# Attention scores in three 64-row products, two row halves at a time

## The reference

```
s_c = q . kc * scale    kc: 63 compressed keys (blocks of 32 tokens, stride 16), mask cmp_end <= t
s_s = q . ks * scale    selected blocks; 16 of 16 blocks are taken, so all tokens <= t
s_w = q . kw * scale    the last 512 tokens
o   = gate0 * softmax(s_c) vc + gate1 * softmax(s_s) vs + gate2 * softmax(s_w) vw
```

## Time and profile before

| | |
|---|---|
| median of 3 runs | 2566.24 us (2565.07 to 2568.8) |
| profiled execution | 2569.07 us, its span 2567.3 us |
| TensorE (PE) busy | 2495.6 us, 97% of the span |
| weight loads (PEld) busy | 2046.7 us, 80% |
| VectorE (DVE) busy | 1711.0 us, 67% |
| ScalarE (ACT) busy | 1053.7 us, 41% |
| GpSimd (POOL) busy | 82.3 us, 3% |
| mean granted TensorE clock | 0.990 |

### The profile page before, as it was taken

How to read it: one execution, slowest core, us unless ns; L and a number is a source line. 1 busy time by engine, 2 the same in 40 slices (tenths; PEclk the granted TensorE clock), 3 DMA queues, 4 the chain that set the end, 5 groups by cost and what they waited for, 6 DMA issues and landing times. The chain is left out here.

```text
span 2567.3 us, 47240 instructions
## 1 busy us (share of the span) xinstructions
PE 2495.6 (97%) x19440; PEld 2046.7 (80%) x19440; DVE 1711.0 (67%) x2707; ACT 1053.7 (41%) x1823; POOL 82.3 (3%) x122
## 2 busy tenths in 40 slices
PE   8999999999899999789999998999999999999998
PEld 7788888888777778777888886877787888888887
DVE  6876676687545455478788777634457866776676
ACT  4322223445433343456655554533443322223443
POOL 0000000000000000011121110000000000000000
PEclk9999999999999999989999999999999999999999
DMA  4323324665432267922212114511121333235464
GB/s 149 101 83 119 118 82 145 207 201 156 99 110 91 69 209 233 256 64 52 56 39 51 46 44 145 200 58 33 66 74 54 128 110 118 89 99 205 143 196 145
DMA packets 279268, 297.91 MB, mean 116 GB/s; under 512 B 75442, under 2 KB 209840, under 8 KB 279088
## 3 DMA queue, kind: packets, MB, share of 16 engines
q1 hardware_dynamic: 276208, 292.59, 36.3%
q10 hardware_dynamic: 2880, 2.75, 0.3%
HBM read 208.67 MB, written 81.36 MB: 113 GB/s over the span
## 5 line engine op out<-in xcount | busy, mean ns | idle before, releaser
L1141 PE MATMUL f_ps<-hi,f_wh 128*128 128x512 f32 x672 | 262.4, 391 | 4.1 <-DVE f_wl L847 4.1
L1143 PE MATMUL f_ps<-hi,f_wl 128*128 128x512 f32 x672 | 262.2, 390 | 0.0
L2586 PE MATMUL f_ps<-hi,f_ahead_h 128*128 128x512 f32 x392 | 163.9, 418 | 0.8 <-PEq L72 0.8
L2588 PE MATMUL f_ps<-hi,f_ahead_l 128*128 128x512 f32 x392 | 153.6, 392 | 0.0
L2587 PE MATMUL f_ps<-one_lo,f_ahead_h 128*128 128x512 f32 x392 | 153.4, 391 | 0.0
L1141 PE MATMUL f_ps<-f_t3h,f_t2h 128*128 128x512 f32 x392 | 152.5, 389 | 0.0
L1142 PE MATMUL f_ps<-f_t3l,f_t2h 128*128 128x512 f32 x392 | 152.5, 389 | 0.0
L1143 PE MATMUL f_ps<-f_t3h,f_t2l 128*128 128x512 f32 x392 | 152.5, 389 | 0.0
L1141 PEld LDWEIGHTS f_ps<-hi,f_wh 128*128 128x128 f32 x672 | 126.6, 188 | 31.3 <-DVE f_wl L847 5.0
L1143 PEld LDWEIGHTS f_ps<-hi,f_wl 128*128 128x128 f32 x672 | 126.5, 188 | 26.3
L1142 PE MATMUL f_ps<-one_lo,f_wh 128*128 128x512 f32 x352 | 137.0, 389 | 0.0
(11 more groups left out here) (586 smaller groups left out, 6595.4 us busy)
## 6 DMA issues: line engine op xcount, KB each, us to landing
act<-one_y SPq DMA_DIRECT2D x30, 512.0 KB, 3.5
f_work<-act SPq DMA_DIRECT2D x30, 512.0 KB, 3.7
act<-y SPq DMA_DIRECT2D x30, 512.0 KB, 3.6
arena<-act SPq DMA_DIRECT2D x30, 512.0 KB, 3.6
one_y<-in_w_in SPq DMA_DIRECT2D x25, 512.0 KB, 4.6
early<-in_ffn_w_gate SPq DMA_DIRECT2D x11, 1024.0 KB, 6.2
early<-in_ffn_w_up SPq DMA_DIRECT2D x11, 1024.0 KB, 8.7
f_raw<-in_ffn_w_gate SPq DMA_DIRECT2D x10, 1024.0 KB, 6.4
```

The costliest lines, as they stand in the source:

```text
L1141: nc.tensor.matmul(out, wh, xh, start=start, stop=False)
L1143: return nc.tensor.matmul(out, wl, xh, start=False, stop=stop)
L2586: nc.tensor.matmul(dense_ps[:, b, cols], w_hi[:, b, k, :], hi[:, k, cols], start=(k == 0), stop=False)
L2588: mm = nc.tensor.matmul(dense_ps[:, b, cols], w_lo[:, b, k, :], hi[:, k, cols], start=False, stop=(k == KD - 1))
```

## The change

1. **Scores.** Tokens of a key block are split into two halves of 64, one in rows 0 to 63 and one in rows 64 to 127 of the key tile; high and low parts of the keys lie side by side in the free dimension. A score step is now three products (high x high, high x low, low x high), each given twice, once for the upper and once for the lower 64 rows, with n x 64 columns each. The low x low product is dropped. The scores of the two halves land in two banks of PSUM.
2. **Masks, minimum, exponential.** VectorE writes masked scores into a new tile `raw` (two buffers), still in two halves; ScalarE's exponential reads it and writes the probabilities in token order. The minimum of step s waits for the exponential of step s - 2; the wait for a free probability tile moves from VectorE to ScalarE (for the compressed part it stays).
3. **Compressed keys.** 64 (63 and a masked one) instead of 63 in a tile `near`, both heads of the pair side by side: one transpose instead of two per unit, one copied block instead of two, and two 64-row products with values that stand in both row halves.
4. **Loads.** `load_keys` issues 16 DMAs with runs of 256 bytes instead of 4; `kc` comes in 4 DMAs instead of 2 and waits for a memset, `vc` in 2 instead of 1.
5. **Recurrence.** VectorE writes T0 = result * m_one at once, L and its mask are gone, and GpSimd has one operation less per chunk.
6. **Planner.** New costs, the moved wait, and a tiling of its own, "rows", for the scores.

```diff
@@ joint_plan
-        event(("score", s), "pe", 0.113 * n + 0.1 + extra, s and ("max", s - 1))
-        event(("max", s), "dve", 0.25 + 1.1 * us + extra, ("score", s), u >= 2 and ("bank", FIRST_FILL[u - 1] - 1))
-        event(("exp", s), "act", 0.4 + us + 2 * extra, ("max", s), s and ("exp", s - 1))
+        event(("score", s), "pe", 0.085 * n + 0.1 + extra / 2, s and ("max", s - 1))
+        event(("max", s), "dve", 0.25 + 1.1 * us + extra, ("score", s), s >= 2 and ("exp", s - 2),
+              u >= 2 and k >= 2 and ("bank", FIRST_FILL[u - 1] - 1))
+        event(("exp", s), "act", 0.4 + us + 2 * extra, ("max", s), s and ("exp", s - 1), u >= 2 and ("bank", FIRST_FILL[u - 1] - 1))
...
-                event(("masked", c), "pool", 4.6, out_of(name))
+                event(("masked", c), "pool", 3.9, out_of(name))
...
-        return e[0] == "values" and "columns" or e[0] == "rw" and e[2] not in ("mean", "var") and "corners" or "whole"
+        return e[0] == "score" and "rows" or e[0] == "values" and "columns" or e[0] == "rw" and e[2] not in ("mean", "var") and "corners" or "whole"
@@ load_keys
-        src = rot[row:row + 2 * DH, :].rearrange("(g d) t -> d g t", d=DH)
-        sp.dma_start(hi[w * CH:(w + 1) * CH, 2 * n:2 * n + 2, :].bitcast(F32), src).then_inc(keys_in, 16)
+        for g in range(2):
+            src = rot[row + g * DH:row + (g + 1) * DH, :].rearrange("d (t r c) -> d r t c", r=2, c=CH)
+            for r in range(2):
+                sp.dma_start(keys_of(hi, n)[r * CH:(r + 1) * CH, w, g].bitcast(F32), src[:, r]).then_inc(keys_in, 16)
@@ score
-                for key, first, n, col in parts:
-                    for m in range(0, max(n, 1), 4):
-                        width = min(4, n - m) * P if n else NB + 1
-                        at = s_ps[:, col + m * P:col + m * P + width]
-                        keys = key[:, g, (first + m) * P:(first + m) * P + width]
-                        nc.tensor.matmul(at, q[:, ring, 0, head % 4, :], keys, start=True, stop=False)
-                        mm = nc.tensor.matmul(at, q[:, ring, 1, head % 4, :], keys, start=False, stop=True)
+                for key, first, n in parts:
+                    for x_, (wq, wk) in enumerate(((0, 0), (0, 1), (1, 0))):
+                        for r in range(2):
+                            if n:
+                                keys, at = key[rows(r), wk, g, first:first + n].rearrange("p t c -> p (t c)"), s_ps[:, r, 0:n * CH]
+                            else:
+                                keys, at = key[rows(r), wk, g], s_ps[:, r, CMP_COL // 2:CMP_COL // 2 + CH // 2]
+                            mm = nc.tensor.matmul(at, q[rows(r), ring, wq, head % 4, :], keys, start=(x_ == 0), stop=(x_ == 2))
@@ turn_probs
-                    for h in range(2):
+                    for h in range(2) if br else ():
                         src = (sel if br == 1 else win)[:, u % 2, h, col:col + P]
                         mm = nc.tensor.transpose(t_ps[:, 2 * m + h, :], src, ident[:])
+                    if not br:
+                        mm = nc.tensor.transpose(t_ps[:, 2 * m, :], near[:, u % 2].rearrange("p h c -> p (h c)"), ident[:])
@@ values
+                        else:
+                            val, prob = vc[rows(h), rows(g)], probT[rows(h), n % 2, 2 * m, :]
+                        mm = nc.tensor.matmul(o_ps[rows(h), u % 2, :], val, prob, start=(f == 0 and m == 0), stop=(br == 0))
@@ exps
-                nc.scalar.activation(slot[:, 0:cols], slot[:, 0:cols], ACT.Exp, bias=bias[:, s % 8, 1:2], scale=-1.0,
+                if u >= 2:
+                    act.wait_ge(flipped, FIRST_FILL[u - 1])
+                nc.scalar.activation(by_token(slot[:, 0:cols]), raw[:, s % 2, :, 0:cols // 2].rearrange("p r (t c) -> p r t c", c=CH), ACT.Exp, bias=bias[:, s % 8, 1:2], scale=-1.0,
@@ masked, on GpSimd
-                    op(j, T0[j][:], L[j][:], over_pairs(m_one[:]), ALU.mult)
+                    op(j, T0[j][:], T0[j][:], over_pairs(eye[:]), ALU.add)
                     op(j, LTm[j][:, 0], GB[j][:, :, 0, :], over_pairs(m_lev[:, 0, :]), ALU.mult)
-                    pool.wait_ge(by_pool[j], through(gn, c, "one"))
-                    op(j, T0[j][:], T0[j][:], over_pairs(eye[:]), ALU.add)
@@ gram_b, on VectorE
-                    op(by_bank(L[j][:]), result(j, 2), all_pairs(m_low[:]), ALU.mult)
+                    op(by_bank(T0[j][:]), result(j, 2), all_pairs(m_one[:]), ALU.mult)
```

More of the change, by code:

```diff
@@ L1306, in shape_tables, with by_halves @@
     tok = np.arange(T).reshape(TT, P)
+    def by_halves(mask):
+        return np.ascontiguousarray(mask.reshape(P, -1, 2, P // 2).transpose(0, 2, 1, 3).reshape(P, 2, -1))
     cmp_ok = (np.arange(NB) * 16 + 31)[None, None, :] <= tok.T[:, :, None]
@@ L1313, in shape_tables @@
         "csin": np.tile(np.concatenate([-cs, cs]), (1, 2)),
[L1315 to L1319, removed]
+        "mask_causal": by_halves(np.concatenate([zero, np.where(t[None, :] > t[:, None], neg, np.float32(0))], 1)),
+        "mask_window": by_halves(np.concatenate([np.where(t[None, :] <= t[:, None], neg, np.float32(0)), zero[:, 0:3 * P],
+                                                 np.where(t[None, :] > t[:, None], neg, np.float32(0))], 1)),
+        "mask_cmp": np.concatenate([np.where(cmp_ok, np.float32(0), neg), np.full((P, TT, 1), neg)], 2).astype(np.float32),
         "mask_row_ok": (t >= 31).astype(np.float32)[:, None],
@@ L1629, in attend_and_recur @@
         padded = core.sem(f"{tag}_padded")
-        gram_in, low_in, eye_in, levels_in, means_in = (core.sem(f"{tag}_{n}_in") for n in ("gram", "low", "eye", "levels", "means"))
+        gram_in, eye_in, levels_in, means_in = (core.sem(f"{tag}_{n}_in") for n in ("gram", "eye", "levels", "means"))
         shapes_in = core.sem(f"{tag}_shapes_in")
@@ L1661, in attend_and_recur @@
         an = numbered(["turn_bk", "ax", *[f"yt{lv}" for lv in range(LEVELS)], "wu", "out", "mean", "square", "var"])
-        gn = numbered(["one", "start", *[f"lev{lv}" for lv in range(LEVELS)]])
+        gn = numbered(["start", *[f"lev{lv}" for lv in range(LEVELS)]])
         def through(numbers, c, name):
@@ L1812, in values @@
                 if n == 0:
-                    pe.wait_ge(values_in, 48)
+                    pe.wait_ge(values_in, 64)
                 if f == 0 and u:
@@ L1954, in copy_probs @@
         def copy_probs(eng, copy, n):
-            m = 2 * len(turns(FILLS[n][0])[FILLS[n][1]])
+            m = sum(2 if br else 1 for br, _, _ in turns(FILLS[n][0])[FILLS[n][1]])
             eng.wait_ge(flipped, n + 1)
@@ L1960, in copy_probs, with by_token, halves @@
             copy(probT[:, n % 2, 0:m, :], t_ps[:, 0:m, :]).then_inc(copied[n % 2], 1)
+        def by_token(x):
+            return x.rearrange("p (t r c) -> p r t c", r=2, c=CH)
+        def halves(x):
+            return x.rearrange("p (r c) -> p r c", r=2)
         def step_of(s):
@@ L2045, in bias_of @@
                 dve.wait_ge(scored, s + 1)
-                if u >= 2:
+                if s >= 2:
+                    dve.wait_ge(exped, steps_through(s - 2))
+                if u >= 2 and k >= 2:
                     dve.wait_ge(flipped, FIRST_FILL[u - 1])
-                mask = window[:] if k >= 2 and i >= 4 else causal[:, T - cols:T]
+                mask = window[:] if k >= 2 and i >= 4 else causal[:, :, (T - cols) // 2:T // 2]
                 nc.vector.memset(gate[:], 0.0)
-                nc.vector.tensor_tensor_reduce(slot[:, 0:cols], s_ps[:, 0:cols], mask, -SCALE, FAR, ALU.add,
+                nc.vector.tensor_tensor_reduce(raw[:, s % 2, :, 0:cols // 2], s_ps[:, :, 0:cols // 2], mask, -SCALE, FAR, ALU.add,
                                                ALU.min, bias[:, s % 8, 1:2]).then_inc(biased, 1)
                 if k >= 2:
-                    at = slice(CMP_COL, CMP_COL + NB)
-                    nc.vector.tensor_tensor_reduce(slot[:, at], s_ps[:, at], cmp_mask[:, i, :], -SCALE, FAR, ALU.add,
+                    nc.vector.tensor_tensor_reduce(halves(near[:, u % 2, k % 2, :]), s_ps[:, :, CMP_COL // 2:CMP_COL // 2 + CH // 2], halves(cmp_mask[:, i, :]), -SCALE, FAR, ALU.add,
                                                    ALU.min, bias[:, s % 8, 0:1]).then_inc(biased, 1)
```

65 lines of the change are left out of this document (33 added, 32 removed).

## The result

The change makes the kernel slower: 2583.34 us (median of 7 runs, 2578.16 to 2597.48) against 2566.24 us (7 runs, 2565.07 to 2568.87), a ratio of 1.0066, 95% interval 1.0053 to 1.0079. The forecast was 2562.0 us, faster; the time lies above its range. The runs also spread five times as wide as before: the fastest has a mean granted TensorE clock of 0.985, the slowest 0.977, against 0.990 of the profiled run of before. The profiled execution after took 2581.49 us, its span 2579.6 us, 12.3 us longer than that of before.

The account below looks back on a forecast made before the run. TensorE was taken to bound the attention stage. Streams -8.4, turns +11.7, order -1.2, compressed block -9.3 and start +3.0 gave -4.2 us, from the median 2566.24 to 2562.0 us, range 2547 to 2574.

Parts of the forecast that it names:

- The start: Beginning of the attention stage: later key loads +2.5 us, small steps at 1.2 GHz +0.5, together +3.0.
- Values of the compressed block: Compressed-key value products: two side-by-side pairs replace four instructions, -3.8 us; sharing the recurrence's tiling in fills, -2.2.
- Small window steps of before: Old window and compressed score steps with turn, priced 0.57, 0.69 and 0.80 us for n = 2, 3, 4.
- The planner's order: Planner sees the new tiling and picks another order, taking back 10 turns between tilings: -1.2 us.
- turns: TensorE's switches between tilings, since scores no longer share one with transposes and means: +11.7 us in the same order.
- The streams of long steps: Score products with overlapping row halves: window steps with n = 5 from 1.02 to 0.87 us, times 32, -4.8 us.
- block: Compressed keys as one block: fewer transposes, paired values and tiling effects, together -9.3 us.
- 32 x 0.12: Compressed block: one transpose less per unit, put at -3.7 us; values as two pairs, put at -3.8.
- 1 (loads don't hold): Score weight loads: two half-height loads cost under 0.11 us, short products nearly free; 2544 us, chance 0.12.
- 2 (halves queue): Score weight loads: the halves' loads go one after the other, 0.22 us a pair; 2618 us, chance 0.06.
- 3: Score products: a row group can't load under its own stream, 30 us more; 2592 us, chance 0.04.
- 4 (the start): Key loads: SP's issues or short packets delay the first product 10 to 14 us; 2570 to 2574, chance 0.14.

Follow-up runs that it names:

- the warm start: The changed kernel with 100 identity products (128x128, fp32) ahead of TensorE's first score step: 2603.17 us, 1.0127 against before.
- the padded kernel: The changed kernel with score products at least 256 columns wide and compressed keys streamed 128 wide: 2575.34 us, 1.0035 against before.
- the old order: The changed kernel with the planner's costs, waits and tilings of the kernel before: 2585.0 us, 1.0061 against before.
- the 256-byte loads: The kernel before with keys loaded by 16 DMAs of 256-byte runs instead of 4 of 4 KB; first score at 1096.69 us instead of 1093.97.

## Why the prediction was wrong

**The step that failed is one half sentence in "The start"**: "+0.5 for small steps (n = 1, 2) at 1.2 GHz, which the 0.11 holds twice as long". It priced the low clock for the stretch in which before had it, about 24 us. The step took the clock for a given and not for something that depends on the work. I had computed myself that steps with n = 1 and 2 become loads with short streams, and all of the first 32 steps are such; from there the question whether the clock would rise at all was one step away. No rival had it either. Measured: some 13 us in the profiled execution, with 47.8 us of low clock from the first score on instead of 14.5. The median lies 1.9 us above that one with the clock at 0.982 instead of 0.984, and over the seven runs the time grows by 19.3 us (2578.16 to 2597.48) while the clock falls from 0.985 to 0.977, that is (0.008 x 2 x 2590) some 41 us more at half speed, 0.47 us lost per us, close to the 0.44 of the warm start. Between after and its padded form it was 13 us for 37.5, 0.35 per us; why less is open, and by the higher rates the clock's part would be 16 to 18 us. The wide spread fits a start that ends earlier or later by chance; only one execution's trace was read.

**Without the clock some 8 us are missing still.** Start aside, the forecast's sum was -7.2 us; measured is 14.1 - 13 = +1 (by the padded kernel 5.4 - 5 = +0.4). How much is missing goes with the clock's part; free of it is the stretch from step 32 to the end, where -4.7 us stand against some -11 by the forecast's terms. Three terms make up most of it.

- *Values of the compressed block, -3.8 and -2.2*: nearly nothing. The timeline of before, then of after:

```profile
1287.47 0.44 PE L1821 MATMUL ar_o_ps<-ar_probT,ar_vc 128*64 128x128 f32 x4
1287.84 0.50 PE L1793 MATMUL ar_s_ps<-hi 128*128 128x512 f32 x1
```

```profile
1119.21 0.48 PE L1842 MATMUL ar_o_ps<-ar_probT,ar_vc 64*64 64x128 f32 x2
1119.23 0.48 PE L1876 MATMUL ar_ps<-ar_YT 64*64 64x64 f32 x4
1119.47 0.42 PE L1842 MATMUL ar_o_ps<-ar_probT,ar_vc 64*64 64x128 f32 x2
...
1281.06 0.44 PE L1842 MATMUL ar_o_ps<-ar_probT,ar_vc 64*64 64x128 f32 x4
1281.42 0.71 PE L1810 MATMUL ar_s_ps<-hi 64*128 64x320 f32 x6
```

Four records take 0.36 us to the next step, 0.37 before. The two heads sit on different rows and columns, but each product is two records of one head, and the second head's begin only 0.26 us after the first's at the low clock (1119.21, 1119.47), when those have gone. Recurrence products, which alternate over four corners, do overlap; this isolated pair does not. That the order of the records is the reason is my reading, and no run alternates them. Summed over the stage the values gave 1.3 to 1.7 us instead of 5.6 in the padded kernel, the old order and the kernel before with block and T0, and nothing in the one with the block alone: 4 us.
- *Small window steps of before*: my prices with the turn were 0.57, 0.69 and 0.80 us for n = 2, 3 and 4; the median steps of before took 0.49, 0.60 and 0.72. With 8 steps of each: 2 us less to give. The 32 steps with n = 5 took 1.00 instead of 1.02, 0.6 us less again.
- *The planner's order, -1.2*: there are 629 turns now against 539. The forecast's came to 539 + 98 - 10 - 18 = 609, and in the order of before there are in fact 619; the new order added ten instead of taking ten back. So the 1.2 us taken back are missing; whether the new order costs more is not shown (0.08% in the kernel before, with an interval that reaches below none, and nothing from step 32 on in after).

The streams of long steps held: after in the order of before takes 368.2 us from step 32 to 127 (444.9 - 76.7) where before takes 372.6, at full clock in both; my terms for these (streams -12, three quarters of turns and block +9 and -7) give -10, and the values and small window steps explain 4.5 of the 6 between. A slip of the forecast beside it: it puts 32 x 0.12 at -3.7 once and at -3.8 once; it is 3.8. Nor did another engine become the bound: from 1113 to 1560 us VectorE is busy for 351 of 447 us, ScalarE for 254.

**The rivals.** 1 (loads don't hold) and 2 (halves queue) fall by the 0.88 us of the n = 5 step; a pair at 0.22 would have made it 1.48. 3 falls by the same number, since a load waiting for its own rows' stream would have added 0.32. The Trainium skill's "TensorE: Matmul & The Clock Gate", "Part 3: Packing small matmuls — row/col tiling", lets loads overlap running products only in another row group; this trace does not bear it out for 64-row products either, where each pair follows the last by about the time of its stream: in the step of 1301.97 us the six products of 320 columns take 0.55 us, where waiting loads would have made them take 0.21 more. 4 (the start) is the one I gave the right sign to, for the wrong reason: first score at 1094.41 us, 0.4 us later than before, while the padded kernel and the 256-byte loads show 1096.9 and 1096.7, in my forecast span. In after the last `kc` load was issued 2.6 us later than before and landed 0.4 us later; why it landed sooner behind its issue is open. The packets were hardly the problem:

```profile
q1 hardware_dynamic: 4298, 1.07, 98.3%
```

This is SP's queue of after from 1066 to 1072 us: 1.07 MB in 6 us, or 178 GB/s, while another queue moved 0.26 MB, 221 GB/s together; with the long runs it was 1.07 MB in 5 us or 214 GB/s, nearly alone. It is 98.3% x 16 x 6 / 4298 = 22 ns a packet of 250 bytes, where 19.7 ns for 296 bytes was forecast. The rule of "DMA: Bandwidth & Descriptors", section "Specifications", in the Trainium skill (512 bytes for line rate) would have doubled the keys' 10 us by my estimate, since the page gives no price; no run here shows that.

## What to carry to other kernels

A change that trades columns for more and shorter products under full-width weights has to be priced with the clock as a result, not as an input: look for stretches where such products would be most of TensorE's work, above all at a stage's start, and give the case that the clock stays low there its own term. Busy share shows none of it; look at the granted clock and at the number of instructions per us. Where an edit bundles several parts, the small part that only removes work (here one transposed block) may be the one worth keeping.

## What the runs showed of the hardware

- A warm start doesn't hold the clock. After 20 us of dense products at 2.4 GHz and 7.5 us of the first steps (PE busy for 5.4) TensorE fell to 1.2 GHz in the changed kernel and stayed there for 54.6 us with PE busy for 53.0; in the kernel before it fell likewise and was back after 6.8 us.
- More columns can be faster: padding products from 64 to 256 columns took 7 us off the kernel (2583.34 to 2576.72 us; ratios 1.0066 and 1.0031 against before measured beside each).
- A weight load of 128 columns holds the next short product by 0.11 us at 2.4 GHz and by 0.22 us at 1.2 GHz.
- Two row halves of 64 rows stream at a time also for float32r and 128 columns of weights: six products of 320 columns and six of 32 in 0.88 us with the turn.
- What it is in the short products that keeps the clock down (idle columns, the load's share, VectorE's and ScalarE's slower pace) is open; no run here tells these apart.
